# Router on a recurrent decoder step: transposing the raw residual rows between a tile's output halves, and one expert pair's transposes behind the first up-projection

## The chip, the cores and the metric

One core of a Trainium2 chip runs the kernel. The metric is the device time of one execution in microseconds, the median of three runs. TensorE multiplies matrices into PSUM, VectorE, ScalarE and GpSimd (POOL) work on vectors, SyncE (SP) issues most transfers; ScalarE (ACT) and POOL issue some too. Each engine runs its own program in order and waits on semaphores. A matmul writes the product of a stationary operand and rows that stream past it; a transpose is such a matmul against an identity.

## What is computed

A decoder layer for 512 prompt rows and 8 sample rows of 1024 numbers, all float32. The part that the change touches comes after the recurrent mixer:

```python
x = x + mix                                  # mix = concat(group A, group B) @ w_out
xn = x * rsqrt(mean(x*x) + 1e-6) * ln2_g     # RMSNorm
p_group = softmax(xn @ wg + bg)              # 4 groups, the best one is taken
logits  = xn @ we + be                       # 8 experts a group, the best two are taken
h = silu(xn @ w1[e]) * (xn @ w3[e])          # 32 experts, 256 wide
y[token] += gate * (h @ w2[e])
out = rmsnorm(x + y) * final_g
```

The weights of the 32 experts are 96 MB and are read once from DRAM; each expert takes the rows that chose it.

## The kernel before, in words

The 520 rows are five tiles, four of 128 rows and one of the 8 sample rows, worked on in the order TILE_ORDER = 0, 4, 1, 2, 3 (tile 4 is the sample tile). A tile's place in this order is its number below.

*Router.* For each place, TensorE multiplies the mixer's output by w_out in two halves of 512 columns (`out_rows`, L1551; the sample tile in a packed form, L1399). VectorE adds each half to the residual rows X (`residual`, L1245, L1249). ScalarE squares the finished rows (L793), takes the root (L795), VectorE inverts it (`invert_root`, L892), ScalarE scales the rows into XS (L797). SP writes XS to DRAM (`xn_rows`, L452) for the later gathers, and TensorE transposes XS in eight pieces (`transpose_rows`, L1374). VectorE copies the transposes out of PSUM times the norm's gain (`evac_xt`, L887), TensorE multiplies them by the router's weights (L1590, the logits "lg"), VectorE adds the bias (L1262) and routes (`route`, L1212 to L1237: some twenty small operations). Of these three PSUM banks turn round, in an order that the list `rotation` fixes.

*What sets the order.* Every engine's program is written out by hand. In the loop over places `i`, TensorE does the first output half of place i, the logits of place i - 2, the second half of place i, the transposes of place i - 1, and waits for these to be written. VectorE does residual, logits of i - 2, residual, copy of the transposes of i - 1, the reciprocal of place i, the routing of place i - 2.

*Positions.* A matmul over all tiles (L1606) counts the rows of each expert, VectorE turns the counts into ranks and a number of rounds (here 1), and every engine loads that number. POOL then raises `round_done` (`s_rdone`, L614), for which VectorE waits at the start of a round. Ten small matmuls (L1671) make a table of row numbers, SRCI (L1316).

*Experts.* Experts go in 16 pairs, 64 rows for each expert. POOL gathers a pair's rows from `xn_rows` (L624 the first two pairs, L597 the others) into T. TensorE transposes them (`turn`, L1617), VectorE copies them out (`xgt`, L1289), TensorE multiplies by w1 and w3 (`up`, L1629), ScalarE and VectorE make silu times gate (L810, `gated`, L1294), TensorE turns this (`turn_h`, L1639) and multiplies by w2 (`down`, L1653), and POOL scatters the result (L609).

*Weights.* SP issues in this order: experts 0 and 1 before the router (L439, L392); the five writes of XS; the final gain (L453); experts 2 and 3, which go where w_out and the mixer's output lay, once the last residual is done; the expert that is kept for the end (L439 to XNT, L465 to XS), once the first two gathers have landed; then, in the loop, w1 and w3 of the expert four further on, whenever an `up` is done with a slot. ScalarE issues w2 after each `down`.

Of the kernel before, what the change touches and what calls it, by code (L numbers as in the profile page):

```python
# [21 lines left out]
ALU = mybir.AluOpType  # L22
# [3 lines left out]
P = 128  # L26
# [4 lines left out]
KD = D // P  # L31
# [30 lines left out]
def rotation():  # L62

    r = []
    for i in range(NT):
        r += [("xt", i, 0), ("xt", i, 1)]
    for name in ("xr", "fx"):
        for m in range(NH):
            r += [(name, m, 0), (name, m, 1)]
            if (name, m) == ("xr", 0):  # L70
                r += [("par", 0), ("par", 1)]
    for m in range(NH):
        r += [("q", m, 0), ("q", m, 1)]
        r += [(g, m, h) for g in ("gx", "ga") for h in range(2)]
    r += [("v", c) for c in TILE_ORDER]
    r += [("xtail",)]
    for s in range(8):
        r += [("gr" if s < 4 else "g", s % 4, 0), ("gr" if s < 4 else "g", s % 4, 1)]
        if s % 2 and s >= 3:
            r += [("mean", (s - 3) // 2)]  # L80
        if s == 6:
            r += [("ost", 0)]
    r += [("mean", 3), ("ost", 1), ("mean", 4), ("htail",)]
    for i in range(NT + 2):
        if i > 1:
            r += [("lg", i - 2)]
        if 1 <= i <= NT:
            r += [("x2t", i - 1, 0), ("x2t", i - 1, 1)]
    r += [("pos",)]
    return {name: (n % NR, n // NR) for n, name in enumerate(r)}  # L90

# [4 lines left out]
def build(nc, x_prompt, x_sample, state_hgrn, state_rglru, state_conv, lower_bounds, ln1_g, w_in,  # L96
# [14 lines left out]
    with ExitStack() as ctx:  # L111
# [257 lines left out]
        def await_ps(eng, name):  # L369
            bank, use = ROT[name]  # L370
            eng.wait_ge(s_written[bank], use + 1)
            return PS[bank]

        def read(ins, name):
            ins.then_inc(s_read[ROT[name][0]], 1)
# [121 lines left out]
        def _(pool):  # L497
# [86 lines left out]
            pool.wait_ge(s_zero, 2)  # L584
            pool.wait_ge(s_xn[0], 16 * 3)
            pool.wait_ge(s_xn[1], 16 * 2)
            pool.wait_ge(s_rnd, 1)
            rounds = pool.value_load(NRND[0:1, 0:1], min_val=1, max_val=MAX_ROUNDS)

# [21 lines left out]
                                        bounds_check=2 * TOK - 1, oob_is_err=False).then_inc(s_ys[p], 16)  # L611


            pool.sem_inc(s_rdone, 1)  # L614
            with pool.Fori(0, rounds) as r:
                base = r * NPAIR
                pool.wait_ge(s_tabr, r + 1)
# [32 lines left out]
        def _(act):  # L650
# [133 lines left out]
            for i, c in enumerate(TILE_ORDER):  # L784
                n = ROWS[c]
                act.wait_ge(s_opr, 2 * i + 2)
                if i == 0:
                    act.wait_ge(s_sout[0], 16 * 4)
                    act.wait_ge(s_sout[1], 16 * 4)
                if i >= 2:  # L790
                    act.wait_ge(s_xst, NT + i - 1)
                    act.wait_ge(s_xn[i % 2], 16 * (i // 2))
                act.activation(XS[0:n, i % 2, :], X[0:n, c, :], ACT.Square, accum_out=SSQ[0:n, c:c + 1]).then_inc(s_ssq, 1)  # L793
                act.wait_ge(s_ssq, NT + i + 1)
                act.activation(RSTD[0:n, c:c + 1], SSQ[0:n, c:c + 1], ACT.Sqrt, scale=1.0 / D, bias=EPSC[0:n, :]).then_inc(s_root, 1)  # L795
                act.wait_ge(s_rstd, NT + i + 1)
                act.activation(XS[0:n, i % 2, :], X[0:n, c, :], ACT.Copy, scale=RSTD[0:n, c:c + 1]).then_inc(s_xs, 1)  # L797
# [68 lines left out]
        def _(dve):  # L866
# [23 lines left out]
            def invert_root(i, c):  # L890
                dve.wait_ge(s_root, i + 1)
                dve.reciprocal(RSTD[0:ROWS[c], c:c + 1], RSTD[0:ROWS[c], c:c + 1]).then_inc(s_rstd, 1)  # L892
# [360 lines left out]


            dve.wait_ge(s_gain[1], 16)
            for i in range(NT + 2):
                if i < NT:
                    residual(i, 0)
                if i > 1:
                    ps = await_ps(dve, ("lg", i - 2))  # L1260
                    n = ROWS[TILE_ORDER[i - 2]]
                    read(dve.tensor_tensor(LG[0:n, i - 2, :], ps[0:n, 0:GROUPS + NE], RB[0:n, :], ALU.add), ("lg", i - 2))  # L1262
                if i < NT:
                    residual(i, 1)
                if 1 <= i <= NT:
                    evac_xt("x2t", i - 1, G2, TILE_ORDER[i - 1])
                if i < NT:
                    invert_root(NT + i, TILE_ORDER[i])
                if i > 1:
                    await_read(dve, ("lg", i - 2))  # L1270
                    route(i - 2, TILE_ORDER[i - 2])
            dve.sem_inc(s_oh, 1)


# [30 lines left out]
            with dve.Fori(0, rounds) as r:  # L1305
# [9 lines left out]
                dve.wait_ge(s_tabs, 2 * r + 2)  # L1315
                dve.tensor_scalar(SRCI[:, 0:NPAIR], DSTI[:, 0:NPAIR], 1, None, ALU.arith_shift_right).then_inc(s_tabr, 1)  # L1316
                xgt(base, 0)
                xgt(base + 1, 1)
                gated(base, 0)
                with dve.Fori(0, NPAIR // 2 - 1) as i:  # L1320
                    for j in range(2):
                        q = base + i * 2 + 1 + j
# [41 lines left out]
        def _(pe):  # L1364
            pe.wait_ge(s_const, 1)

            def transpose_rows(name, i, c):

                n = ROWS[c]
                xv = XS[0:n, i % 2, :].rearrange("t (p k) -> t k p", k=KD)  # L1370
                for j in range(2):
                    ps = claim(pe, (name, i, j))
                    for k in range(4):
                        ins = pe.transpose(ps[:, k * P:k * P + n], xv[:, 4 * j + k, :], IDENT[0:n, 0:n])  # L1374
                    written(ins, (name, i, j))

            for i in range(NT):
                pe.wait_ge(s_xs, i + 1)
                transpose_rows("xt", i, i)
                bank, use = ROT[("xt", i, 1)]  # L1380
                pe.wait_ge(s_written[bank], use + 1)
                pe.sem_inc(s_xst, 1)
# [195 lines left out]
            pe.wait_ge(s_y, NH + 1)  # L1578
            out_rows(0, 0, part=1)
            out_rows(0, 1, part=1)  # L1580
            for i in range(NT + 2):
                if 0 < i < NT:
                    out_rows(i, 0)
                if i > 1:
                    c = TILE_ORDER[i - 2]
                    n = ROWS[c]
                    ps = claim(pe, ("lg", i - 2))
                    await_read(pe, ("x2t", i - 2, 1))
                    for k in range(KD):
                        ins = pe.matmul(ps[0:n, 0:GROUPS + NE], XNT[:, k, c * P:c * P + n], WR[:, k, :],  # L1590
                                        start=(k == 0), stop=(k == KD - 1))
                    written(ins, ("lg", i - 2))
                if 0 < i < NT:
                    out_rows(i, 1)
                if 1 <= i <= NT:
                    pe.wait_ge(s_xs, NT + i)
                    transpose_rows("x2t", i - 1, TILE_ORDER[i - 1])
                    bank, use = ROT[("x2t", i - 1, 1)]
                    pe.wait_ge(s_written[bank], use + 1)
                    pe.sem_inc(s_xst, 1)  # L1600


            ps = claim(pe, ("pos",))
# [57 lines left out]
            with pe.Fori(0, rounds) as r:  # L1661
# [15 lines left out]
                pe.sem_inc(s_pmu, 1)  # L1677
                half_n = r * (NPAIR // 2)
                turn(base, 0, half_n)
                turn(base + 1, 1, half_n)  # L1680
                up(base, 0, r, 0)
                turn_h(base, 0)

                def two_pairs(i, last=False):
# [41 lines left out]
```

## Time and profile before

| | us |
|---|---|
| median of 3 runs | 661.05 |
| lowest and highest | 660.33, 662.53 |
| span of the profiled execution | 656.5 |
| TensorE busy | 510.5 |
| VectorE busy | 230.2 |
| ScalarE busy | 142.6 |
| POOL busy | 79.2 |

The span goes from the first to the last instruction of the profiled execution; its own time outside the span isn't on the page. The mixer ends near 247, the router's tiles run from there to 322, the positions and the table to 331, the expert pairs to 624, and the final norm to 656. TensorE's busy time is the largest, but a busy TensorE is not one at its peak: its granted clock is 0.88 of full on the mean, and its share differs from stage to stage. So the rows below are those of the router and of the first expert pairs, in order of time; the DMA share is the mean busy share of the core's 16 transfer engines.

### The profile page before, as it was taken

To read this page: it belongs to the slowest core of one execution; us is meant where nothing else is said; L and a number is where in the kernel's file an instruction comes from. 1 tells how busy PE (TensorE), PEld (TensorE's weight loads), DVE (VectorE), ACT (ScalarE), POOL (GpSimd) and SP (SyncE) were. 2 spreads that over 40 slices of the span, in tenths; PEclk is the share of its full clock that TensorE was granted. 3 is DMA by queue.
4 is the path that set the end of the run, shared out by engine and by line. 5 is a ranking of instruction groups with operands and counts; after the bars stand their busy time and mean duration, and the time that the engine had idled before them with its cause. 6 is when DMAs were issued, how large, how long until landed. Compare 5 with 4: busy or idle time off the path is not lost. (4 is left out here: it accounts for less than half of the span.)

```text
span 656.5 us, 6560 instructions
## 1 busy us (share of the span) xinstructions
PE 510.5 (78%) x2320; PEld 296.6 (45%) x2320; DVE 230.2 (35%) x519; ACT 142.6 (22%) x267; POOL 79.2 (12%) x129
## 2 busy tenths in 40 slices
PE   3999999999999989999459839395684929478800
PEld 3788888358888733545333313132231313123200
DVE  3353112694987565233721111111020111101158
ACT  7211044704256352212100000000010000001123
POOL 4000000100211211000030111102011111101014
PEclk9899999999999979999559869788795969779955
DMA  9403110412341439210969999999999999969263
GB/s 300 151 0 129 57 72 12 152 53 77 100 165 64 144 122 308 116 44 22 342 230 331 375 376 337 388 336 394 336 369 376 355 379 331 398 198 381 82 280 130
DMA packets 90494, 144.62 MB, mean 220 GB/s; under 512 B 6489, under 2 KB 72197, under 8 KB 85856
## 3 DMA queue, kind: packets, MB, share of 16 engines
q1 hardware_dynamic: 79608, 100.57, 45.9%
q10 hardware_dynamic: 3888, 28.31, 10.6%
q0 software_dynamic: 6976, 15.44, 7.1%
q8 instruction: 14, 0.23, 0.2%
q14 instruction: 8, 0.07, 0.0%
HBM read 137.49 MB, written 15.10 MB: 232 GB/s over the span
## 5 line engine op out<-in xcount | busy, mean ns | idle before, releaser
L1390 PE MATMUL ps<-XNT,WC 128*128 128x260 f32 x640 | 144.8, 386 | 1.2 <-PE ps L1390 0.6
L1390 PEld LDWEIGHTS ps<-XNT,WC 128*128 128x128 f32 x640 | 121.9, 192 | 23.3 <-issue 4.0
L1629 PE MATMUL ps<-WC,XRC 128*64 128x512 f32 x128 | 69.0, 700 | 66.7 <-DMA GY<-in_exp_w 66.7
L1294 DVE TENSOR_TENSOR XRC<-ps,XRC 128x256 f32<-128x256 f32 x16 | 6.8, 424 | 184.2 <-ACT XRC L810 184.2
L1629 PE MATMUL ps<-GY,XRC 128*64 128x512 f32 x128 | 69.0, 701 | 0.0
L1629 PEld LDWEIGHTS ps<-WC,XRC 128*64 128x64 f32 x128 | 19.8, 162 | 107.7 <-issue 107.6
L1629 PE MATMUL ps<-SLOT,XRC 128*64 128x512 f32 x240 | 59.0, 617 | 2.4 <-DMA SLOT<-in_exp_w 2.4
L1551 PE MATMUL ps<-WC,GY 128*128 128x512 f32 x128 | 58.6, 611 | 1.0 <-DVE GY L1184 0.6
L810 ACT ACTIVATE XRC<-ps 128x256 f32<-128x256 f32 x16 | 6.1, 383 | 209.2 <-PE ps L1629 209.2
L609 POOL DMA_INDIRECT expert_rows<-T,SIDX x16 | 16.1, 1008 | 236.9 <-ACT T L824 220.1
L1551 PEld LDWEIGHTS ps<-WC,GY 128*128 128x128 f32 x128 | 24.4, 196 | 29.4 <-issue 28.2
L1629 PEld LDWEIGHTS ps<-SLOT,XRC 128*64 128x64 f32 x240 | 18.1, 142 | 37.4 <-issue 34.1
L1617 PE MATMUL ps<-IDENT,T 128*128 128x128 f32 x128 | 19.3, 299 | 14.0 <-DMA T<-xn_rows,GIDX 12.7
L1289 DVE TENSOR_TENSOR XRC<-ps,G 128x512 f32<-128x512 f32 x32 | 20.6, 685 | 25.8 <-PE ps L1617 25.8
L1653 PE MATMUL ps<-WC,XRC 128*64 128x512 f32 x128 | 28.9, 593 | 0.6 <-ACT XRC L814 0.6
L1653 PE MATMUL ps<-SLOT,XRC 128*64 128x512 f32 x120 | 28.9, 592 | 0.0
L1439 PE MATMUL ps<-WC,XNT 128*128 128x512 f32 x64 | 28.2, 596 | 0.3 <-DVE Vt L1022 0.3
L1299 DVE COPY T<-ps 128x512 f32<-128x512 f32 x16 | 11.1, 691 | 44.3 <-PE ps L1653 44.3
L1617 PEld LDWEIGHTS ps<-IDENT,T 128*128 128x128 f32 x128 | 16.8, 197 | 15.6 <-issue 13.7
L824 ACT ACTIVATE T<-ps 128x512 f32<-128x512 f32 x16 | 9.6, 597 | 64.7 <-issue 50.3
L1374 PE MATMUL ps<-IDENT,XS 128*128 128x128 f32 (+1 forms) x80 | 13.6, 320 | 10.4 <-ACT XS L669 10.3
L1629 PEld LDWEIGHTS ps<-GY,XRC 128*64 128x64 f32 x128 | 19.9, 163 | 0.0
(273 smaller groups left out, 587.7 us busy)
## 6 DMA issues: line engine op xcount, KB each, us to landing
SLOT<-in_exp_w SPq DMA_DIRECT2D x32, 1024.0 KB, 12.4
WC<-in_exp_w SPq DMA_DIRECT2D x18, 1024.0 KB, 13.3
GY<-in_exp_w SPq DMA_DIRECT2D x16, 1024.0 KB, 17.7
WC<-in_exp_w ACTq DMA_DIRECT2D x14, 1024.0 KB, 8.5
SLOT<-in_exp_w ACTq DMA_DIRECT2D x13, 1024.0 KB, 8.8
WC<-in_w_in SPq DMA_DIRECT2D x6, 2048.0 KB, 9.2
WC<-in_w_out SPq DMA_DIRECT2D x2, 2048.0 KB, 7.8
X<-in_x_prompt SPq DMA_DIRECT2D x4, 512.0 KB, 4.7
```

The source lines that it names most:

```text
L609: pool.indirect_dma_start(out=ye_dram, out_offset=bass.IndirectOffsetOnAxis(ap=SIDX[:, p, :].bitcast(U32), axis=0), in_=YO[p], in_offset=None,
L824: act.activation(YO[p][:, 0:512], PS[5][:, :], ACT.Copy).then_inc(s_ya, 1)
L1289: dve.tensor_tensor(XGT[p][:, 4 * j:4 * j + 4, :], PS[j][:, :].rearrange("p (k t) -> p k t", k=4), bc(G2[:, 4 * j:4 * j + 4], 2, P), ALU.m ...
L1294: dve.tensor_tensor(HG[p], PS[2 + p][:, FE:2 * FE], HS[p], ALU.mult).then_inc(s_hg, 1)
L1299: dve.tensor_copy(YO[p][:, 512:1024], PS[6][:, :]).then_inc(s_yd, 1)
L1374: ins = pe.transpose(ps[:, k * P:k * P + n], xv[:, 4 * j + k, :], IDENT[0:n, 0:n])
L1390: ins = pe.matmul(ps[:, 0:HALF], WC[:, j % 2, k, m * P:(m + 1) * P], XNT[:, k, hf * HALF:(hf + 1) * HALF], start=(k == 0), stop=(k == KD - 1))
L1439: ins = pe.matmul(ps[:, :], XNT[:, k, c * P:(c + 1) * P], WC[:, 1, k, :], start=(k == 0), stop=(k == KD - 1))
L1551: ins = pe.matmul(ps[:, :], rows, weights, start=(j == 0), stop=(j == 2 * NH - 1), skip_group_check=True)
L1617: ins = pe.transpose(PS[k // 4][:, (k % 4) * P:(k % 4 + 1) * P], xv[:, k, :], IDENT[:])
L1629: ins = pe.matmul(PS[2 + p][at:at + CAP, :], XGT[p][:, k, at:at + CAP], weights[two][0][:, k, :], start=(k == 0), stop=(k == KD - 1), tile ...
L1653: ins = pe.matmul(PS[5 + half][at:at + CAP, :], HT[p][:, j, at:at + CAP], weights[two][1][:, j, half * 512:(half + 1) * 512], start=(j == ...
```

## The change

The router's transposes no longer wait for the norm. TensorE transposes the residual rows X themselves, once both halves' residuals are added, and the reciprocal root is multiplied into the logits as VectorE reads them (one operation: times RSTD, plus the bias). The transposes of place i - 1 stand between the two output halves of place i, the logits of place i - 1 right behind the second half; TensorE's wait for the transposes to be written is gone. The list `rotation` names two transposes and one logits for each tile in turn, on the same three banks as before. On VectorE the copy of the transposes and the reciprocal of place i - 1 stand between the two residuals of place i, and the routing of place i - 1 behind them. ScalarE still squares, takes the root and scales into XS, and SP still writes XS for the gathers; SP's program is unchanged.

In the expert stage TensorE does the first pair's `up` before the second pair's `turn`, and VectorE the first pair's `gated` before the second pair's `xgt`. POOL raises `round_done` before it waits for the number of rounds. The diff's pieces are POOL's, ScalarE's, VectorE's (two) and TensorE's (three), in this order.

```diff
             pool.wait_ge(s_xn[1], 16 * 2)
+            pool.sem_inc(s_rdone, 1)
             pool.wait_ge(s_rnd, 1)
...
-            pool.sem_inc(s_rdone, 1)
...
                 if i >= 2:
-                    act.wait_ge(s_xst, NT + i - 1)
                     act.wait_ge(s_xn[i % 2], 16 * (i // 2))
...
-            for i in range(NT + 2):
+            for i in range(NT + 1):
                 if i < NT:
                     residual(i, 0)
-                if i > 1:
-                    ps = await_ps(dve, ("lg", i - 2))
-                    n = ROWS[TILE_ORDER[i - 2]]
-                    read(dve.tensor_tensor(LG[0:n, i - 2, :], ps[0:n, 0:GROUPS + NE], RB[0:n, :], ALU.add), ("lg", i - 2))
+                if i > 0:
+                    evac_xt("x2t", i - 1, G2, TILE_ORDER[i - 1])
+                    invert_root(NT + i - 1, TILE_ORDER[i - 1])
                 if i < NT:
                     residual(i, 1)
-                if 1 <= i <= NT:
-                    evac_xt("x2t", i - 1, G2, TILE_ORDER[i - 1])
-                if i < NT:
-                    invert_root(NT + i, TILE_ORDER[i])
-                if i > 1:
-                    await_read(dve, ("lg", i - 2))
-                    route(i - 2, TILE_ORDER[i - 2])
+                if i > 0:
+                    c = TILE_ORDER[i - 1]
+                    n = ROWS[c]
+                    dve.wait_ge(s_rstd, NT + i)
+                    ps = await_ps(dve, ("lg", i - 1))
+                    read(dve.scalar_tensor_tensor(out=LG[0:n, i - 1, :], in0=ps[0:n, 0:GROUPS + NE], scalar=RSTD[0:n, c:c + 1],
+                                                  in1=RB[0:n, :], op0=ALU.mult, op1=ALU.add), ("lg", i - 1))
+                    await_read(dve, ("lg", i - 1))
+                    route(i - 1, c)
...
                 xgt(base, 0)
+                gated(base, 0)
                 xgt(base + 1, 1)
-                gated(base, 0)
...
+            def turn_rows(i):
+
+                c = TILE_ORDER[i]
+                pe.wait_ge(s_opr, 2 * i + 2)
+                transpose_rows("x2t", i, c, X[0:ROWS[c], c, :])
...
+            for i in range(1, NT):
+                out_rows(i, 0)
+                turn_rows(i - 1)
+                out_rows(i, 1)
+                logits(i - 1)
+            turn_rows(NT - 1)
+            logits(NT - 1)
...
                 turn(base, 0, half_n)
+                up(base, 0, r, 0)
                 turn(base + 1, 1, half_n)
-                up(base, 0, r, 0)
                 turn_h(base, 0)
```

How the instructions stand now. First TensorE at the start of the router, in the kernel before: the sample tile's output halves are the rows `WC,GY 8x512`, transposes are the rows with IDENT, logits those with WR.

```order
L1399 MATMUL ps6<-WC,GY 8x512 x8
L1399 MATMUL ps7<-WC,GY 8x512 x8
L1374 MATMUL ps1<-IDENT,XS 128x128 x4
L1374 MATMUL ps2<-IDENT,XS 128x128 x4
L1551 MATMUL ps4<-WC,GY 128x512 x8
L1590 MATMUL ps0<-WR,XNT 128x36 x8
L1551 MATMUL ps5<-WC,GY 128x512 x8
```

The same place on TensorE in the changed kernel:

```order
L1396 MATMUL ps6<-WC,GY 8x512 x8
L1371 MATMUL ps1<-IDENT,X 128x128 x4
L1371 MATMUL ps2<-IDENT,X 128x128 x4
L1396 MATMUL ps7<-WC,GY 8x512 x8
L1590 MATMUL ps0<-WR,XNT 128x36 x8
L1548 MATMUL ps4<-WC,GY 128x512 x8
```

Place 0's transposes have moved between the sample tile's halves, and its logits ahead of the next tile's first output half.

Next VectorE at the end of the router, before: the last residual's second half (X), copies of transposes (XNT), the reciprocal, the first operation of a routing, the reading of logits (`ps0,RB`).

```order
L1245 TENSOR_TENSOR X<-ps5,X 128x512
L887 TENSOR_TENSOR XNT<-ps1,G2 128x4x128
L887 TENSOR_TENSOR XNT<-ps2,G2 128x4x128
L892 RECIPROCAL RSTD<-RSTD 128x1
L1212 COPY Vt<-Vt 128x4
...
L1262 TENSOR_TENSOR Vt<-ps0,RB 128x36
L887 TENSOR_TENSOR XNT<-ps1,G2 128x4x128
L887 TENSOR_TENSOR XNT<-ps2,G2 128x4x128
L1212 COPY Vt<-Vt 128x4
```

The same place on VectorE in the changed kernel:

```order
L1241 TENSOR_TENSOR X<-ps5,X 128x512
L1265 SCALAR_TENSOR_TENSOR Vt<-ps0,RSTD,RB 128x36
L1208 COPY Vt<-Vt 128x4
...
L1233 TENSOR_TENSOR Vt<-Vt 128x32
L883 TENSOR_TENSOR XNT<-ps1,G2 128x4x128
L883 TENSOR_TENSOR XNT<-ps2,G2 128x4x128
L888 RECIPROCAL RSTD<-RSTD 128x1
L1265 SCALAR_TENSOR_TENSOR Vt<-ps0,RSTD,RB 128x36
```

The last tile's copy stood between the reading of the logits before it and their routing; it now stands behind that routing, with the last reciprocal behind it.

Last TensorE at the start of the expert stage, before: two turns (IDENT,T), the first up (SLOT,XRC), the turn of its result.

```order
L1617 MATMUL ps<-IDENT,T 128x128 x8
L1614 ISA
L1617 MATMUL ps<-IDENT,T 128x128 x8
L1622 REGISTER_ALU
L1625 REGISTER_ALU
L1625 ISA
L1629 MATMUL ps<-SLOT,XRC 64x512 x16
L1639 MATMUL ps<-IDENT,XRC 128x128 x2
```

The same place in the changed kernel:

```order
L1617 MATMUL ps<-IDENT,T 128x128 x8
L1622 REGISTER_ALU
L1625 REGISTER_ALU
L1625 ISA
L1629 MATMUL ps<-SLOT,XRC 64x512 x16
L1614 ISA
L1617 MATMUL ps<-IDENT,T 128x128 x8
L1639 MATMUL ps<-IDENT,XRC 128x128 x2
```

The second turn has moved behind the first up.

## Rows read from the trace of the kernel before

**Rows 1.** The page's costliest groups: busy, mean ns, idle before and its releaser

```profile
L1629 PE MATMUL ps<-WC,XRC 128*64 128x512 f32 x128 | 69.0, 700 | 66.7 <-DMA GY<-in_exp_w 66.7
```

**Rows 2.** Stretches: length, busy time of each engine, granted clock, DMA share, GB/s

```profile
312.00:332.00 20.00, 8.16 (x62) 7.00 (x60) 12.69 (x65) 1.69 (x4) 0.56 (x2) 0.50 1.03 349
332.00:340.00 8.00, 2.70 (x12) 2.31 (x13) 1.29 (x2) 0.00 (x0) 3.08 (x5) 0.50 0.34 96
350.00:352.00 2.00, 2.00 (x14) 1.46 (x16) 0.53 (x1) 0.38 (x1) 0.00 (x0) 1.00 0.37 63
```

**Rows 3.** SP's transfers in order of time: start, length of the issue, what

```profile
311.66 1.72 SPq L439 DMA_DIRECT2D WC<-in_exp_w  x2
...
338.21 1.25 SPq L439 DMA_DIRECT2D XNT<-in_exp_w  x2
...
349.48 0.60 SPq L439 DMA_DIRECT2D SLOT<-in_exp_w  x1
```

**Rows 4.** POOL in order of time: the second gather

```profile
333.82 1.05 POOL L624 DMA_INDIRECT T<-xn_rows,GIDX  x1 [0.87 <-POOL GIDX L621]
```

**Rows 5.** Gathers from issue to landing: the first two (L624), then the other fourteen (L597)

```profile
DMA to landing us min/median/max: 4.2/4.2/4.3
...
DMA to landing us min/median/max: 7.6/8.2/9.2
```

**Rows 6.** TensorE in the router, in order of time: start, length, what, idle before

```profile
253.66 3.62 PE L1399 MATMUL ps<-WC,GY 128*8 128x512 f32 x32
257.40 1.16 PE L1374 MATMUL ps<-IDENT,XS 128*128 128x128 f32 x8
258.71 7.10 PE L1551 MATMUL ps<-WC,GY 128*128 128x512 f32 x16
265.65 1.87 PE L1590 MATMUL ps<-WR,XNT 128*128 128x36 f32 x16
...
307.01 1.05 PE L1374 MATMUL ps<-IDENT,XS 128*128 128x128 f32 x8
309.24 1.95 PE L1590 MATMUL ps<-WR,XNT 128*128 128x36 f32 x16 [1.18 <-DVE XNT L887]
...
314.57 3.60 PE L1590 MATMUL ps<-WR,XNT 128*128 128x36 f32 x16 [2.17 <-DVE XNT L887]
322.20 0.98 PE L1606 MATMUL ps<-Vt,LTRI 128*128 128x192 f32 x2 [4.04 <-DVEq L1272]
```

**Rows 7.** VectorE in the router, in order of time

```profile
256.08 5.70 DVE L1249 TENSOR_TENSOR X<-ps,X 8x512 f32<-8x512 f32 x8
...
307.21 0.69 DVE L1245 TENSOR_TENSOR X<-ps,X 128x512 f32<-128x512 f32 x1 [6.75 <-PE ps L1551]
307.82 1.28 DVE L887 TENSOR_TENSOR XNT<-ps,G 128x512 f32<-128x512 f32 x2
...
318.27 0.20 DVE L1262 TENSOR_TENSOR Vt<-ps,RB 128x36 f32<-128x36 f32 x1 [0.45 <-PE ps L1590]
```

**Rows 8.** ScalarE's scaling of the last tile

```profile
309.64 1.15 ACT L797 ACTIVATE XS<-X,RSTD 128x1024 f32<-128x1024 f32 x1 [0.23 <-DVE RSTD L892]
```

**Rows 9.** TensorE in the expert stage, in order of time

```profile
335.92 1.97 PE L1617 MATMUL ps<-IDENT,T 128*128 128x128 f32 x8 [6.13 <-DMA T<-xn_rows,GIDX]
339.26 1.97 PE L1617 MATMUL ps<-IDENT,T 128*128 128x128 f32 x8 [1.38 <-DVE XRC L1289]
341.17 7.71 PE L1629 MATMUL ps<-SLOT,XRC 128*64 128x512 f32 x32
349.85 0.50 PE L1639 MATMUL ps<-IDENT,XRC 128*128 128x128 f32 x2 [0.97 <-DVE XRC L1294]
...
365.61 8.78 PE L1629 MATMUL ps<-SLOT,XRC 128*64 128x512 f32 x32 [2.39 <-DMA SLOT<-in_exp_w]
...
403.78 7.09 PE L1629 MATMUL ps<-SLOT,XRC 128*64 128x512 f32 x32
```

**Rows 10.** Waits from 255 to 360: total us, times, longest

```profile
DVE Vt L1311 <- POOLq L588: 1.5, 1, 1.5
```

More of the change, by code:

```diff
@@ L83, in rotation @@
     r += [("mean", 3), ("ost", 1), ("mean", 4), ("htail",)]
-    for i in range(NT + 2):
-        if i > 1:
-            r += [("lg", i - 2)]
-        if 1 <= i <= NT:
-            r += [("x2t", i - 1, 0), ("x2t", i - 1, 1)]
+    for i in range(NT):
+        r += [("x2t", i, 0), ("x2t", i, 1), ("lg", i)]
     r += [("pos",)]
@@ L1255, in _ @@
             dve.wait_ge(s_gain[1], 16)
-            for i in range(NT + 2):
+            for i in range(NT + 1):
                 if i < NT:
                     residual(i, 0)
-                if i > 1:
-                    ps = await_ps(dve, ("lg", i - 2))
-                    n = ROWS[TILE_ORDER[i - 2]]
-                    read(dve.tensor_tensor(LG[0:n, i - 2, :], ps[0:n, 0:GROUPS + NE], RB[0:n, :], ALU.add), ("lg", i - 2))
+                if i > 0:
+                    evac_xt("x2t", i - 1, G2, TILE_ORDER[i - 1])
+                    invert_root(NT + i - 1, TILE_ORDER[i - 1])
                 if i < NT:
                     residual(i, 1)
-                if 1 <= i <= NT:
-                    evac_xt("x2t", i - 1, G2, TILE_ORDER[i - 1])
-                if i < NT:
-                    invert_root(NT + i, TILE_ORDER[i])
-                if i > 1:
-                    await_read(dve, ("lg", i - 2))
-                    route(i - 2, TILE_ORDER[i - 2])
+                if i > 0:
[7 more added lines that the diff above has]
+                    route(i - 1, c)
             dve.sem_inc(s_oh, 1)
@@ L1365, in _, with transpose_rows @@
             pe.wait_ge(s_const, 1)
-            def transpose_rows(name, i, c):
+            def transpose_rows(name, i, c, rows):
                 n = ROWS[c]
-                xv = XS[0:n, i % 2, :].rearrange("t (p k) -> t k p", k=KD)
+                xv = rows.rearrange("t (p k) -> t k p", k=KD)
                 for j in range(2):
@@ L1378, in _ @@
                 pe.wait_ge(s_xs, i + 1)
-                transpose_rows("xt", i, i)
+                transpose_rows("xt", i, i, XS[0:ROWS[i], i % 2, :])
                 bank, use = ROT[("xt", i, 1)]
@@ L1580, in _, with logits @@
             out_rows(0, 1, part=1)
[L1581 to L1600, printed above, removed]
+            def turn_rows(i):
+                c = TILE_ORDER[i]
+                pe.wait_ge(s_opr, 2 * i + 2)
+                transpose_rows("x2t", i, c, X[0:ROWS[c], c, :])
+            def logits(i):
+                c = TILE_ORDER[i]
+                n = ROWS[c]
+                ps = claim(pe, ("lg", i))
+                await_read(pe, ("x2t", i, 1))
+                for k in range(KD):
+                    ins = pe.matmul(ps[0:n, 0:GROUPS + NE], XNT[:, k, c * P:c * P + n], WR[:, k, :],
+                                    start=(k == 0), stop=(k == KD - 1))
+                written(ins, ("lg", i))
+            for i in range(1, NT):
[5 more added lines that the diff above has]
+            logits(NT - 1)
             ps = claim(pe, ("pos",))
```

## The prediction

> **What bounds the kernel now.** I read the page's costliest groups first. In the expert stage, the last half of the span, TensorE's longest wait is for weights: 66.7 us in 7 waits at L1629, all for GY, which holds the last of four experts' weights [rows 1]. The stream of expert weights sets the pace there, so a microsecond of that stretch is worth a microsecond only where the transfers idle. They idle in two places [rows 2]: from 332 to 340 (share 0.34; the prefetch of experts 2 and 3, issued from 311.66 on [rows 3], has run out) and from 350 to 352 (share 0.37). What opens the stream for good is the load of the kept expert at 338.21, and what holds that is the landing of the first two gathers: the second is issued at 333.82 [rows 4], an early gather lands 4.2 us after its issue [rows 5], and SP goes on 0.2 later. What holds the gathers is the router. So the question is when, after the change, three things happen: the prefetch of experts 2 and 3, the second gather, the first load of the loop (349.48 [rows 3]).
>
> In the router I read TensorE's and VectorE's order of time [rows 6, 7]. TensorE goes from one output half to the next without a hole until 307.01; from there to the positions' matmul at 322.20 the router's last tiles are a chain through VectorE, 15.2 us long.
>
> Names: T is the eight transposes of a tile, lg its eight logit matmuls, numbered by place in TILE_ORDER (place 1 is the eight sample rows); "out 2 first" is a tile's output half.
>
> **The start of the router (+1.25).** T0 now stands between the sample tile's halves and lg0 right behind them, ahead of out 2 first. The two halves take 3.62 from 253.66 [rows 6], so the first ends at 255.5, T0 (1.05, as at 307.01) at 256.5, the second half at 258.3. lg0 needs the copy of T0 out of PSUM, and on VectorE that copy now stands behind the sample tile's first residual: four of the eight small additions that take 5.70 [rows 7], so 2.85. VectorE starts 0.2 after TensorE ends a half (307.01 against 307.21), so residual to 258.5, copy 1.28 to 259.8, lg0 at 259.95: TensorE stands idle for 1.65 us, with all output matmuls queued behind. lg0 takes 1.87, and the next matmul starts 0.16 before its end (258.71 plus 7.10 against 265.65): out 2 first starts at 261.65, not 258.71. Of these 2.95 us, 1.7 is lg0, which came later before; 1.25 is new.
>
> **The middle (+0.75).** T1 and T2 no longer end in a wait for their own writes: T0 ends at 258.56 and the next matmul starts at 258.71, 0.15 each, so -0.3. T3 moves ahead of the last output half: +1.05. The last half ends at 309.0 instead of 307.0. Within the middle the added waits cost nothing: T waits for the residual of the same tile, which VectorE does under the 7 us of an output half, and lg for a copy long done.
>
> **The tail (router's end +1.6).** The change takes ScalarE's square, root and scale from between the last residual and T4; that chain runs from 307.21 to about 310.8 today. But VectorE's program order puts something else there: lg3's read and routing, then T4's copy, then lg4. From 309.0: lg3 1.95; 0.1 to VectorE (314.57 plus 3.60 against 318.27 [rows 6, 7]); read and routing 3.75 (318.27 to 322.20 is 3.93 with the hand-over); copy 1.28; 0.1; lg4 3.60, since the clock is at 0.50 there now [rows 2] and TensorE will have stood nearly 5 us; 0.1; read, routing and hand-over 3.93. That is 14.8, so the positions start at 323.8 instead of 322.2. Today lg4's 3.6 us lie beside a routing; now nothing does. Bound from below: lg4 as fast as lg0, -1.73.
>
> **The prefetch (+6.6).** The scaled rows still go to DRAM for the gathers, but the reciprocal that ScalarE's scaling waits for now stands behind T4's copy, so behind routing 3: 309.0 + 1.95 + 0.1 + 3.75 + 1.28 = 316.1. With 0.15 for it and 1.15 for the scaling [rows 8] the last rows are scaled at 317.4, against 310.8. SP writes these rows before it loads experts 2 and 3; those follow the scaling by 0.87 (311.66): 318.3. The six loads end near 338.7 instead of 332.
>
> **The gathers (kept expert +3.4).** They are issued 1.6 later, the second at 335.4, now in the middle of these loads instead of behind them. Ends: 4.2 from issue to landing, as now, puts the kept expert's load at 339.8 (+1.6); the slowest of the later gathers, all of which meet weight loads, took 9.2 [rows 5] (+6.6). The later gathers' median is 8.2, but the loads end some 3 us into the second gather's time, so I take 6.0, nearly midway: +3.4.
>
> The Trainium skill, page "DMA: Bandwidth & Descriptors", section "Queues, rings and completion order", says that each transfer engine takes turns between the queues, a packet from each. By that a gather beside loads should land almost as soon as one alone, and the sum would be 1.8 less. The rows speak against it (8.2 against 4.2); it is a rival below.
>
> **The two swaps in the expert stage (0).** The first up now starts where the second turn did, 339.26 for 341.17 [rows 9], 1.91 earlier. Half of that is lost again if the clock rises at the same moment, since 1.91 us more of it run at half clock: it gains 0.95. That moves the first load of the loop, not the kept expert's. Today the load is issued 13.6 after the first turn starts (335.92 to 349.48), 0.5 ahead of the stream's running dry near 350; the hole of 350 to 352 loses 2 x 0.63 = 1.3 us. After the change: first gather landed near 340.3, load at 340.3 + 12.6 = 352.9, stream dry at 350 + 3.4 = 353.4, again 0.5 ahead. So the hole stays: 0, with -1.3 (closed) to +1.0 (the clock rises later). The second turn, the third gather and gated's new place are covered by the weights' wait. POOL's earlier round_done removes the 1.5 us that the profile puts to L588 [rows 10] only in name: VectorE loads the same round count after the same semaphore. I take 0, bound -1.5.
>
> **TensorE's clock (+1.7).** It is 1.2 GHz at half and 2.4 at full. It fell to half near 312, after an idle 1.18 us, thin logit matmuls and eight transposes [rows 6, 2]. From 258.3 to 261.65 stands the same mix: 1.65 us idle, then lg0. If it falls there, the output halves behind run at half for a while. The price is that of the up at 365.61, which follows an idle of 2.39: 8.78 against 7.09 with none [rows 9], 1.7. Ends: 0 (an idle of 0.97 before 349.85 left it full), and 3.4, where lg0 takes 3.60 too. I take 1.7, the nearest row. It shifts prefetch, gathers and stream alike.
>
> **The rivals.** The profiled span is 656.5 (the table above); 4.55 us lie around it up to the median of 661.05, and I keep them.
> Forecast: 661.05 + 3.4 + 1.7 = 666.1.
> *The clock holds.* For it: full clock through all the router's body until now. Against it: the fall near 312. 661.05 + 3.4 = 664.4.
> *The gathers aren't slowed, and the clock holds* (not slower). The late prefetch then fills the idle 332 to 340, the kept expert comes 1.6 later, the first turn at 337.5, the loop's first load at 350.1, 1.5 ahead of the dry point 351.6 instead of 0.5, so the hole loses 1.0: 661.6. It decides where a gather beside loads lands within about 5 us; the steady gathers speak against. With the clock falling it is 663.3.
> *The change does less than it says*: the sample tile's residual is out of the way before T0's copy. The code's order forbids it; 661.05 + 3.4 - 1.25 = 663.2.
> *Faster* would need lg4 at full clock, quick gathers and a closed hole together: near 659.
>
> **How the numbers follow.** A measurement of this kernel tells about 0.3%, 2 us, from no change: 659.1 to 663.0. Forecast 0.40; clock holds 0.22; quick gathers with the clock held 0.10, with it fallen 0.13; less than it says 0.06; faster 0.09. Slower by over 0.3%: 0.40, 0.22, 0.08 of the 0.13 and 0.04 of the 0.06, 0.74; within: 0.17; faster: 0.09. The range goes from the quick gathers, 661.5, to a gather at nearly 9 us or the dearer clock, 668.5; some 2 in 10 stay outside.
>
> **What would show it.** A TensorE hole of about 1.6 us between the sample tile's second half and lg0, with VectorE in the small additions; a granted clock of half soon after (or not: the second case); experts 2 and 3 loaded from 318 to 320 on instead of 311.7; routing 3 ahead of T4's copy, lg4 with VectorE idle; the kept expert's load 3 to 5 us later; the hole near 353 still there. I am wrong if the prefetch starts before 315, or if the stream's end doesn't move with the kept expert's load.

## The result, and the profile after

The changed kernel takes 668.95 us (median of four executions: 665.60, 666.75, 671.15, 671.48) against 661.26 for the kernel before beside it: ratio 1.0116, 95% interval 1.0075 to 1.0158. It is slower, as forecast, but by 7.7 us instead of 5.05, and 0.45 above the top of the range. The profiled execution is that of 666.75, with a span of 665.0.

The four times lie in two pairs 5 us apart, and the profiled execution is one of the lower pair. TensorE, in order of time, at the start of the router and from its last output half on (start us, us, engine, line, operation, what idled ahead of it and what ended that); lines are now 2 to 4 lower than in [rows 6]:

```profile
255.55 1.90 PE L1396 MATMUL ps<-WC,GY 128*8 128x512 f32 x16
257.38 1.16 PE L1371 MATMUL ps<-IDENT,X 128*128 128x128 f32 x8
258.47 1.90 PE L1396 MATMUL ps<-WC,GY 128*8 128x512 f32 x16
261.83 1.95 PE L1590 MATMUL ps<-WR,XNT 128*128 128x36 f32 x16 [1.45 <-DVE XNT L883]
263.61 7.11 PE L1548 MATMUL ps<-WC,GY 128*128 128x512 f32 x16
...
310.44 1.87 PE L1590 MATMUL ps<-WR,XNT 128*128 128x36 f32 x16
312.14 1.12 PE L1371 MATMUL ps<-IDENT,X 128*128 128x128 f32 x8
317.67 3.60 PE L1590 MATMUL ps<-WR,XNT 128*128 128x36 f32 x16 [4.41 <-DVE XNT L883]
325.36 0.98 PE L1606 MATMUL ps<-Vt,LTRI 128*128 128x192 f32 x2 [4.09 <-DVEq L1269]
...
343.63 1.97 PE L1617 MATMUL ps<-IDENT,T 128*128 128x128 f32 x8 [10.68 <-DMA T<-xn_rows,GIDX]
347.16 8.99 PE L1629 MATMUL ps<-SLOT,XRC 128*64 128x512 f32 x32 [1.56 <-DVE XRC L1286]
```

The router begins 1.89 later than in [rows 6] (sample tile at 255.55 for 253.66), ahead of everything that the change touches; more on that below. In what follows, a time "by S" is counted from this begin. So counted, the wait of 1.45 before lg0 is the one that was forecast, out 2 first stands 8.06 behind the sample tile's begin (forecast 8.0), and the positions 69.81 (before 68.54, [rows 6]).

SP's queue (the transfers that SyncE issues), the same way; it answers to [rows 3]:

```profile
306.12 13.01 SPq L449 DMA_DIRECT2D xn_rows<-XS  x2
...
319.64 1.73 SPq L436 DMA_DIRECT2D WC<-in_exp_w  x2
...
344.03 1.26 SPq L436 DMA_DIRECT2D XNT<-in_exp_w  x2
...
356.75 5.99 SPq L436 DMA_DIRECT2D SLOT<-in_exp_w  x4
```

Experts 2 and 3 are loaded from 319.64 (before 311.66), the kept expert from 344.03 (338.21), the loop's first load comes at 356.75 (349.48). The reason is in the order on VectorE and ScalarE: the last copy and reciprocal come behind routing 3, and the scaling of the last rows behind them.

```profile
316.24 1.29 DVE L883 TENSOR_TENSOR XNT<-ps,G 128x512 f32<-128x512 f32 x2
317.44 0.15 DVE L888 RECIPROCAL RSTD<-RSTD 128x1 f32<-128x1 f32 x1
```
```profile
317.63 1.15 ACT L793 ACTIVATE XS<-X,RSTD 128x1024 f32<-128x1024 f32 x1 [4.79 <-DVE RSTD L888]
```

The first two gathers are issued at 334.79 and 336.98 and now meet those loads. Their time to landing, and then the stretch in which the weight stream stands dry in the expert stage (stretch, length, five busy times with counts, granted clock, DMA share, GB/s):

```profile
DMA to landing us min/median/max: 7.0/7.8/8.7
```
```profile
355.00:359.00 4.00, 3.00 (x19) 1.80 (x16) 1.71 (x3) 0.77 (x2) 0.64 (x2) 1.00 0.11 22
```

The first gather takes 8.7 and the second 7.0 instead of 4.2 for an early one [rows 5]. The hole, the dry stretch of the weight stream, costs 4 x 0.89 = 3.6 us of transfers, where it cost 1.3 in 350 to 352 [rows 2].

The spans differ by 8.5 us, and four pieces make it up: the router's begin 1.89, the kept expert's load counted from there 3.93 (88.48 for 84.55), from it to the loop's first load 1.45 (12.72 for 11.27), and the rest 1.23.

**The base.** An execution's time is its span plus 1.75 us in the changed kernel (666.75 and 665.0), and within 0.1 in every kernel below. By that the span of 656.5 belongs to a time of 658.25, 2.8 below the median of 661.05. The 4.55 us "around the span" of my prediction are thus 1.75 around it and 2.8 by which the profiled execution lay below the median. Two kernels below keep the old router: their sample tile begins at 255.61 and 256.36. So the later begin of 255.55 is no part of the change. In all twelve profiles the begin lies anywhere from 253.66 to 258.74; in three of them the output half ahead of the sample tile takes 8.83 instead of 7.13 (granted clock 0.66 in 249 to 254 of one of them), so TensorE's clock also falls in places that no edit touches. Times of the kernel before range from 657.95 to 664.65 in the comparisons below, so single executions 3 us apart mean little.

### The profile page after: what moved, and what is told of

It reads as the page before. It is cut to its first block and busy times, and to the rows that moved or that the text cites. A ratio compares the mean times of both kernels' runs of the same rounds, so it can differ in the third digit from the quotient of the medians.

```text
span 665.0 us, 6560 instructions
## 1 busy us (share of the span) xinstructions
PE 509.5 (77%) x2320; PEld 296.2 (45%) x2320; DVE 230.6 (35%) x519; ACT 142.7 (21%) x267; POOL 79.2 (12%) x129
## 5 line engine op out<-in xcount | busy, mean ns | idle before, releaser
L1436 PEld LDWEIGHTS ps<-WC,XNT 128*128 128x128 f32 x64 | 11.9, 190 | 16.0 <-issue 14.9
```

Source lines behind the costliest of these rows:

```text
L1436: ins = pe.matmul(ps[:, :], XNT[:, k, c * P:(c + 1) * P], WC[:, 1, k, :], start=(k == 0), stop=(k == KD - 1))
```

## The experiments

Names: lg is a tile's eight logit matmuls and T its eight transposes, numbered by place as in the prediction; S is the begin of the sample tile's first matmul in a profile, K the issue of the kept expert's load (XNT), F the loop's first load (SLOT). Positions are those of the matmul with LTRI.

### The last scaled rows written from ScalarE's queue

SP then has nothing to wait for ahead of experts 2 and 3; nothing else moves.

```diff
-            for i, c in enumerate(TILE_ORDER):
+            for i, c in enumerate(TILE_ORDER[:-1]):
                 sp.wait_ge(s_xs, NT + i + 1)
...
+            c = TILE_ORDER[-1]
+            act.wait_ge(s_xs, 2 * NT)
+            act.dma_start(xn_dram[c * P:c * P + ROWS[c], :], XS[0:ROWS[c], (NT - 1) % 2, :]).then_inc(s_xn[(NT - 1) % 2], 16)
```

> The changed kernel, with one edit: ScalarE, not SP, issues the write of the last tile's scaled rows, so that SP's prefetch of experts 2 and 3 no longer stands behind it. Theory (late prefetch): it starts when the last residual is done, near 312 instead of 319.6, and has ended when the gathers are issued; both gathers land 4.2 us after their issue instead of 8.7 and 7.0, the kept expert's load comes some 2.6 earlier, and the first up, 4.5 earlier, closes the wider hole behind it: 664.5 where the changed kernel has 668.95 (4 runs). Rival (the router's later end and the clock are the whole loss): the router is untouched, so 668 to 669.

Measured: 664.4 (five executions, 662.6 to 666.6), 1.0063 [1.0039, 1.0088], as the first theory has it. SP's queue, and the first two gathers:

```profile
310.83 1.27 SPq L436 DMA_DIRECT2D WC<-in_exp_w  x2
...
340.78 1.25 SPq L436 DMA_DIRECT2D XNT<-in_exp_w  x2
...
351.24 6.59 SPq L436 DMA_DIRECT2D SLOT<-in_exp_w  x4
```
```profile
DMA to landing us min/median/max: 3.4/3.8/4.2
```

The prefetch starts 8.8 us earlier, is over when the gathers are issued, and these land in half the time. K - S is 85.75 instead of 88.48, F - K 10.46 instead of 12.72. So the later prefetch costs time not by its own lateness (in the changed kernel TensorE first uses these weights at 359.7, and the transfers' share is down to 0.20 by 342 to 343) but through the gathers that it now meets. What is left: K - S stands 1.3 behind that of the two kernels with the old router (84.4), and this is the router's later end, since the positions still stand 69.81 behind S. The profiled execution, the lowest of the five at 662.6, is 1.5 behind the median of the kernel before; the median is 3.3 behind, and what the other four executions lost is in no profile.

### The last copy and reciprocal ahead of routing 3

```diff
-                if i > 0:
+                if 0 < i < NT:
                     evac_xt("x2t", i - 1, G2, TILE_ORDER[i - 1])
...
+                    if i == NT - 1:
+                        evac_xt("x2t", i, G2, TILE_ORDER[i])
+                        invert_root(NT + i, TILE_ORDER[i])
                     await_read(dve, ("lg", i - 1))
                     route(i - 1, c)
```

> The changed kernel, with the copy of the last tile's transposes and its reciprocal ahead of the routing of the tile before on VectorE. Theory: the last logits run beside that routing again, the positions start 2.9 us earlier, the prefetch 2.7 earlier, the gathers stand to it as they do now: 666. Rival (the order on VectorE doesn't matter, since the gathers wait for the loads anyway): within 1 of the changed kernel's 668.95.

Measured: 664.05 (ten executions, 661.99 to 668.62), 1.0051 [1.0022, 1.0079], 2 us better than the theory. TensorE in its profile, which is of a slower execution, 668.15:

```profile
265.01 1.95 PE L1593 MATMUL ps<-WR,XNT 128*128 128x36 f32 x16 [1.44 <-DVE XNT L883]
266.79 8.81 PE L1551 MATMUL ps<-WC,GY 128*128 128x512 f32 x16
...
319.17 1.95 PE L1593 MATMUL ps<-WR,XNT 128*128 128x36 f32 x16 [1.03 <-DVE XNT L883]
326.50 0.98 PE L1609 MATMUL ps<-Vt,LTRI 128*128 128x192 f32 x2 [5.39 <-DVEq L1272]
```

lg4 now lies beside routing 3 and, after an idle 1.03 instead of 4.41, runs at full clock: 1.95 instead of 3.60. This execution also shows what the lower pair of the changed kernel didn't: behind lg0's wait, which is the same 1.44, out 2 first takes 8.81 instead of 7.11; the clock has fallen (0.55 granted in 267 to 270), and it costs 1.7. Without that the positions would stand 66.1 behind S, 3.7 earlier than in the changed kernel. The gathers still take 7.4 and 7.7.

### T0 and lg0 moved out of the way at the router's start

TensorE does both sample halves, then T0, out 2 first, lg0, T1; VectorE does both sample residuals, then T0's copy, and reads lg0 behind out 2 first's residual. TensorE's part of the edit:

```diff
-            for i in range(1, NT):
+            out_rows(1, 0)
+            out_rows(1, 1)
+            turn_rows(0)
+            for i in range(2, NT):
                 out_rows(i, 0)
+                if i == 2:
+                    logits(0)
                 turn_rows(i - 1)
```

> The changed kernel, with the first tile's transposes behind the sample tile's second half and its logits behind the next tile's first half, as before the change. Theory: the 1.45 us idle and the thin stretch between 260.3 and 263.6 go, and with them the executions in which the clock falls there: all runs within 2 us of each other, near 665. Rival (the two groups of times, 666 and 671, come from something else): both groups stay, each 1.2 lower.

Measured: 666.2 (nine executions, 661.88 to 667.62), 1.0063 [1.0036, 1.0090]. Half a hit: the times near 671 are gone, but the spread is 5.7 us, not 2, and the level is 1 above the theory. Its profile has no wait ahead of T0 or lg0 and full clock behind (out 2 first 7.03); positions stand 67.93 behind S, 1.9 less than in the changed kernel. S itself is late here, 257.39, since the output half ahead of the sample tile ran at half clock, a piece of code that no edit touches.

### The wait ahead of lg0 made longer

VectorE does both sample residuals ahead of T0's copy, and nothing else changes.

```diff
                     residual(i, 0)
+                if i == 1:
+                    residual(i, 1)
                 if i > 0:
                     evac_xt("x2t", i - 1, G2, TILE_ORDER[i - 1])
...
-                if i < NT:
+                if i < NT and i != 1:
                     residual(i, 1)
```

> The changed kernel with one more delay ahead of lg0 and nothing else: VectorE does both of the sample tile's residuals (2.85 us each) ahead of T0's copy, so TensorE should stand idle for about 4.3 us instead of 1.45, and everything behind it comes 2.85 later. Theory (the idle stretch ahead of lg0 is what lets TensorE's clock fall in the executions of the changed kernel near 671, and not in those near 666): with the longer stretch it falls nearly every time: out 2 first takes 8.8 to 9.6 us instead of 7.1 in the profile, and all runs lie in the upper group moved by 2.85, 672.5 to 675. Rival (the two groups have nothing to do with that stretch): the profile shows full clock behind lg0, and the runs lie at 668.5 and at 674.

Measured: 674.31, four executions within 0.7 (673.71 to 674.38), 1.0191 [1.0167, 1.0215]. TensorE in its profile, and the clock there (the last but two column):

```profile
264.80 2.72 PE L1592 MATMUL ps<-WR,XNT 128*128 128x36 f32 x16 [4.38 <-DVE XNT L883]
267.33 9.72 PE L1550 MATMUL ps<-WC,GY 128*128 128x512 f32 x16
```
```profile
264.00:268.00 4.00, 3.20 (x17) 3.04 (x18) 1.05 (x5) 2.48 (x4) 0.00 (x0) 0.72 1.05 402
268.00:270.00 2.00, 2.00 (x3) 0.67 (x2) 1.73 (x12) 0.00 (x0) 0.00 (x0) 0.50 0.41 166
270.00:274.00 4.00, 4.00 (x8) 1.70 (x7) 1.32 (x8) 0.00 (x0) 0.00 (x0) 0.68 0.00 0
```

The times lie where the theory put them, and out 2 first at 9.72, just above its 9.6. The wait is 4.38, lg0 2.97 later; the clock falls within lg0, and lg0 and out 2 first together take 3.4 us longer than at full clock (2.72 for 1.95, 9.72 for 7.11). With 2.97 taken off, the four times are 670.7 to 671.4, beside the upper pair of the changed kernel (671.15 and 671.48). So with a long wait the clock seems to fall every time (one profile shows it, and the other three times agree), with 1.45 only sometimes.

### The old order of turn and up in the changed kernel, and the new one in the kernel before

```diff
                 turn(base, 0, half_n)
-                up(base, 0, r, 0)
                 turn(base + 1, 1, half_n)
+                up(base, 0, r, 0)
```

This is TensorE's part. It is the changed kernel's edit taken back (and likewise gated behind the second xgt on VectorE); the other run is the kernel before with the same lines the other way.

> The changed kernel with the second pair's turn ahead of the first up again, and the second pair's copy ahead of gated. Theory: the first up starts 1.9 later but with the clock nearer to full; the loop's first load comes 0 to 1 later, and the time is the changed kernel's 668.95 plus 0 to 1. Rival (the swap widened the hole before the loop's first load, by starting the up at half clock): 1.5 to 2 less, 667.

> The kernel before with one part of the change alone: in the expert stage the first up ahead of the second turn, and gated ahead of the second xgt. Theory (the swaps cost nothing where they stand beside the old router): the first up starts 1.9 earlier, the loop's first load comes 0.5 to 1 earlier than 349.48 if the start of the router is the same, and the time is that of the kernel before within 1 us: 660 to 661.5. Rival (the swaps are what makes the hole of the weight stream longer in the changed kernel): the loop's first load comes 1 to 2 later, and the time is 662 to 663.

Measured: changed kernel without the swap 669.25 (four executions, 665.33 to 672.16), 1.0106 [1.0063, 1.0150]; kernel before with it 660.72, 0.9993 [0.9967, 1.0018]. Both lie where the first theories put them, and neither is told apart from its base. SP's queue without the swap, then the kernel before with it and its dry stretch:

```profile
348.82 1.26 SPq L436 DMA_DIRECT2D XNT<-in_exp_w  x2
362.73 5.86 SPq L436 DMA_DIRECT2D SLOT<-in_exp_w  x4
```
```profile
340.79 1.25 SPq L439 DMA_DIRECT2D XNT<-in_exp_w  x2
342.14 1.63 SPq L465 DMA_DIRECT2D XS<-in_exp_w  x1
352.10 6.12 SPq L439 DMA_DIRECT2D SLOT<-in_exp_w  x4
```
```profile
352.00:355.00 3.00, 2.00 (x16) 1.69 (x14) 1.70 (x3) 0.38 (x1) 1.28 (x3) 1.00 0.27 89
```

F - K is 13.91 without the swap and 12.72 with it in the changed kernel: it brings the first load 1.2 earlier. In the kernel before it is 11.31 with it, and 11.27 [rows 3] or 12.10 (the run below) without; of the half to whole microsecond that the expectation gave, 0 to 0.8 is there. The hole stays, 3 x 0.73 = 2.2 us in this stretch; over 4 us (351 to 355, share 0.40) it is 2.4. The run below, without the swap, has 2.5 in the same 4 us (share 0.38). So the swap is not what made the hole longer, and the 1.3 of [rows 2] is a low case for the old router. The run without it also shows the clock's fall at the same place with the changed kernel's own router (lg0's wait again 1.45):

```profile
263.50 2.88 PE L1590 MATMUL ps<-WR,XNT 128*128 128x36 f32 x16 [1.45 <-DVE XNT L883]
266.19 9.56 PE L1548 MATMUL ps<-WC,GY 128*128 128x512 f32 x16
```

That is 0.93 + 2.45 = 3.4 us more than in the changed kernel's profile. This execution took 672.16, 5.4 more than the changed kernel's; its S, 257.23, is also 1.7 later, and the two together come to 5.1. The other three times, 665.33, 668.17 and 670.32, fall into no two groups, so the clock at lg0 isn't all that spreads them.

### round_done earlier in the kernel before

```diff
             pool.wait_ge(s_xn[1], 16 * 2)
+            pool.sem_inc(s_rdone, 1)
             pool.wait_ge(s_rnd, 1)
...
-            pool.sem_inc(s_rdone, 1)
```

> The kernel before with one part of the change alone: GpSimd counts s_rdone up earlier in its program. Theory: the time of the kernel before, 660.5 to 661.5. Rival (the 1.5 us that the profile puts to the later place are real and lie on the way to the first gathers): 659.5.

Measured: 662.25 (four executions, 661.70 to 663.03), 1.0012 [0.9988, 1.0035], 0.75 above the theory's range and no faster than its base. The profile has the same wait of 1.5 us on VectorE, now put to an instruction of TensorE's queue (L1609). The 1.5 us of [rows 10] are a name for a wait and not a cost of this place.

### Everything taken back that was lost

All of the above together: the reordered start, the last copy ahead of routing 3, the write from ScalarE's queue, the old order of turn and up. Then two kernels that split it: the two reorders of the router alone (the start, and the last copy), and all but the old order of turn and up.

> The changed kernel with what each experiment so far showed to be lost taken back in one: T0 behind the sample tile's second half and lg0 behind out 2 first (no idle stretch), the last transposes' copy and reciprocal ahead of routing 3, the last tile's scaled rows written from ScalarE's queue, and the old order of turn and up. Theory (late prefetch, stall at the router's start and the longer tail are the whole loss, and the two transposes' saved waits remain): positions at 319 to 321 where the kernel before has 322.2, experts 2 and 3 loaded from about 309, first gathers land within 4.5 us, all runs within 3 us of each other, time 658 to 660. Rival (something else in the change costs 2 to 3 us as well, for instance the logits' later scaling by the root): 662 to 664.

> The changed kernel with the router's two reorders alone: T0 behind the sample tile's second half and lg0 behind out 2 first, and the last transposes' copy and reciprocal ahead of routing 3; the last scaled rows are written by SP and the first up stays ahead of the second turn. Positions then come about 64.2 us after the sample tile's halves begin, as in the kernel with all four edits, and the last rows are scaled 58 us after that start, so experts 2 and 3 are loaded about 4 us later than there. Theory (what the gathers still meet of the prefetch is a loss of its own): the first gathers land 6 us or more after their issue instead of 3.5 to 4.0, and the time is 660 to 662. Rival (once the router is shorter, the place of the write is worth nothing): gathers at 4.5 us or less, 657 to 658.5.

> The faster kernel (all four edits, 657.38) with the changed kernel's order of the expert stage put back in: the first up ahead of the second turn, gated ahead of the second xgt. Theory (the swap is worth nothing in either direction, as it was in the kernel before and in the changed kernel): 656.5 to 658.5, the loop's first load as far behind the kept expert's as there, 11.2 us, within 1 us. Rival (the swap pays where gathers are quick, as in the run with the write moved, where that distance was 10.5): 655 to 656.5.

| kernel | us | ratio to before | positions - S | K - S | F - K | first gathers land after |
|---|---|---|---|---|---|---|
| before, its profile | 661.05 | 1 | 68.54 | 84.55 | 11.27 | 4.2 for an early one |
| changed | 668.95 | 1.0116 [1.0075, 1.0158] | 69.81 | 88.48 | 12.72 | 8.7, 7.0 |
| two reorders | 660.87 | 0.9995 [0.9966, 1.0023] | 64.20 | 82.99 | 11.81 | 7.1 to 8.3 |
| all four | 657.38 | 0.9941 [0.9914, 0.9968] | 64.21 | 79.92 | 11.18 | 3.5 to 4.0 |
| all but the old turn and up | 657.28 | 0.9922 [0.9899, 0.9946] | 64.20 | 80.01 | 10.27 | 3.5 to 4.1 |

Each row's ratio is to the kernel before measured beside it (661.26, 662.36, 661.54 and 662.36, from the second row down). The times came out by the first theories, save that the kernel with all four lies 0.6 below its expected 658 and spreads over 5.6 us (654.68 to 660.25), not 3. In the last row F - K is 10.27, at the edge of the theory's range and nearer to the rival's 10.5: the swap brings the first load 0.9 earlier there, and the time doesn't show it. TensorE at the router's end with all four, and SP's queue:

```profile
308.71 1.87 PE L1612 MATMUL ps<-WR,XNT 128*128 128x36 f32 x16
310.42 1.12 PE L1393 MATMUL ps<-IDENT,X 128*128 128x128 f32 x8
312.56 2.68 PE L1612 MATMUL ps<-WR,XNT 128*128 128x36 f32 x16 [1.03 <-DVE XNT L887]
319.91 0.98 PE L1633 MATMUL ps<-Vt,LTRI 128*128 128x192 f32 x2 [4.67 <-DVEq L1291]
```
```profile
309.63 1.27 SPq L436 DMA_DIRECT2D WC<-in_exp_w  x2
...
335.62 1.25 SPq L436 DMA_DIRECT2D XNT<-in_exp_w  x2
```

From lg3 to the positions it is 11.2 us, where the kernel before takes 15.2 from its last transposes at 307.01 to 322.20 [rows 6]. That is what reading the residual rows can bring: T4 follows lg3 at once and lg4 lies beside routing 3. The changed kernel has the same operations and gives this away by the place of three of them (the last two copies and the last reciprocal). With the two reorders alone the gathers still meet the loads, and the time is that of the kernel before; who writes the last rows is worth the other 3.6 us (660.87 to 657.28; the two kernels differ in nothing else). The gathers of these two:

```profile
DMA to landing us min/median/max: 7.1/7.7/8.3
```
```profile
DMA to landing us min/median/max: 3.5/3.8/4.1
```

Both kernels at 657.3 are faster than either kernel of the case.

## Why the prediction was wrong in size

The mechanism was right: a late prefetch that the first gathers meet. Two terms of the sum failed. The 0 for the hole of the weight stream should have been 1.1 to 2.3, because its premise on the first gather's landing was wrong; and the clock's 1.7 is no constant, but 0, 1.7 or 3.4 by the execution. The gathers' 3.4 was 0.5 too small.

**Start of the router, +1.25: right.** Wait 1.45 for a forecast 1.65, out 2 first 8.06 behind S for 8.0.

**Middle and tail, +0.75 and positions +1.6: nearly right.** Positions 1.27 later by S. T4's copy behind routing 3 and lg4 at 3.60 with VectorE waiting, as said.

**Prefetch, +6.6: right.** 319.64 - 1.89 = 317.75, forecast 318.3.

**The gathers, +3.4 from "I take 6.0, nearly midway": too small, 3.93 measured.** The kept expert's load hangs on the second gather, which took 7.0 for 6.0 and was issued 0.3 earlier than forecast. The loads ended later than thought: the DMA share is 0.89 in 340 to 341, 0.61 in the next microsecond and 0.20 in 342 to 343, so about 5 us into the second gather's time and not 3; it landed at 344.0, the first at 343.5. The rival of quick gathers is refuted for a gather beside loads, and its value is what one gets by parting them: 3.4 to 4.2 when the write leaves SP's queue.

**"The two swaps (0) ... so the hole stays": the step that failed without any clock.** The swaps did about what the text says of them (F earlier by 1.2 in the changed kernel and by 0 to 0.8 in the kernel before, for 0.95; no time gained or lost). What failed is the premise in the same paragraph, "first gather landed near 340.3": less the 1.89 it is 341.6, because of the 8.7. (The 340.3 doesn't follow from the text's own 6.0 either: 331.62 + 1.6 + 6.0 is 339.2.) The stream ran dry where forecast (about 355.1 - 1.89 = 353.2, forecast 353.4), but F came at 354.9 instead of 352.9: 1.3 of these 2.0 us are the gather's, and 0.7 lie between its landing and F, 13.3 for 12.6. The hole grew from 1.3 in the profile before, or 2.5 in the other kernel with the old router and no swap, to 3.6: +1.1 to +2.3 for a 0 with a bound of +1.0.

These two make the lower pair: 661.3 + 3.9 + 1.1 = 666.3, or 667.5 with 2.3; measured 665.6 and 666.75.

**TensorE's clock, +1.7: right that it can fall there, wrong in size, and it is no constant.** In the changed kernel's profile it doesn't fall at lg0. Where it does, in runs with the same wait (1.44 and 1.45), it cost 1.7 once and 3.4 once, and 3.4 with the longer wait. The 3.4 was an end of the term; the nearest row, which I chose, was that of an up behind an idle stretch [rows 9], without lg0's own loss and with less of the next half at half clock. 666.3 + 3.4 = 669.7 for 671.2 and 671.5; the 1.5 between is not placed. That the upper pair of the changed kernel itself had this fall was not seen in a profile of it; it rests on the run with the longer wait (all times there lie near the upper pair plus 2.97) and on the runs without a wait, where no time above 668 is left. A later begin of the router, which moves by 5 us between profiles, is a rival for a part of it that no run here rules out.

**The other rivals.** That the change does less than it says fell with the wait of 1.45 in the place foretold. Faster needed lg4 at full clock, quick gathers and a closed hole; the changed kernel has none of the three (3.60, 8.7, 3.6 us), and the kernel that got the first two by reordering is the faster one.

The median of 668.95 lies between the pairs, and another four executions could move it by a few us. The range ended at a slow gather or a dear clock, not both, and left the hole out. Slower was right; whether the probabilities of the two clock cases (0.40 falling, 0.22 holding) were good, four executions can't say.

## What to carry to other kernels

When an edit delays a prefetch, look not at its own lateness but at what it will now run beside: here a late prefetch slowed two gathers to twice their time, and these held everything behind them. A step that takes work off a chain is worth nothing until the program order of the other engines lets the rest of the chain close up: the same operations gave +7.7 us in one order and -4 in another, with the last write issued from another engine. And before a profile's own time is taken as the base, compare its span with the span and time of another execution, so that one that lies below the median isn't read as typical.

## What the runs showed of the hardware

One of the first two gathers, issued while weight loads are under way, lands 6.7 to 8.8 us after its issue, in all six kernels in which it met them (the changed one and the five experiments that leave the last write on SP's queue behind the new router), and 3.4 to 4.2 in the three in which the loads had ended. The Trainium skill, page "DMA: Bandwidth & Descriptors", section "Queues, rings and completion order", has each transfer engine take turns between queues by packets. The prediction read from this that a gather beside loads loses little; the page gives no figure for that, and these runs don't bear the reading out: the gather loses about as much time again as it takes alone. In all six kernels both gathers land 0.6 to 2.5 us after the transfers' share first falls under 0.5, so these runs don't tell a gather that is slowed throughout from one that is held until the loads are nearly done.

The same TensorE program up to there, with the same idle stretch (1.44 to 1.46 us) ahead of the same 16 thin matmuls, kept its granted clock in two profiles (1.00 in the microseconds behind it) and lost it in two (0.55 and 0.54), for 1.7 and 3.4 us. An idle 4.38 there made the time both longer and steadier (four executions within 0.7 us, against 6 for the changed kernel). This short idle stretch thus had no fixed cost. That it is what spreads the executions is not shown: nine executions without it still lie 5.7 us apart, and nineteen of the kernel before 6.7.
